# A two-layer decoder step: the seam from attention heads to the output units in another order, and the last memory mix inside the first key unit

## The chip, the core and the metric

The kernel runs on one core of a Trainium2 chip. Its engines are TensorE (PE in the rows; PEld is its weight load), VectorE (DVE), ScalarE (ACT), GpSimd (POOL) and SyncE (SP), which here issues DMAs. The metric is the device time of one execution in microseconds (us).

## What is computed

A trunk of two layers with width 1024 handles 544 tokens: 512 of a prompt and 32 of eight requests (four each). The part that matters here, cut from the reference:

```python
# layer 1, after the residual stream x of layer 0
k_new = rope(rmsnorm(x) @ w_k); v_new = rmsnorm(x) @ w_v
z = rmsnorm(x) @ w_in[1]; z_mix, z_mem = z[..., :768], z[..., 768:]
q = rope(z_mix)
p = softmax(q k / 8)                      # two score maps for each of 6 heads
o = (p[0] - lam * p[1]) @ v
o = rmsnorm(o, subln) * (1 - lam_init)    # per head, 128 wide
x = x + concat(o, memattn(z_mem)) @ w_out[1]
x = x + relu(rmsnorm(x) @ w_mlp1[1])**2 @ w_mlp2[1]
```

## The kernel before, in words

All matrix products with weights run in "units". A unit is one 128-wide slice of output features for all 544 tokens: eight contraction tiles (kt), for each of them three products (high weights by high and low operand, low weights by high operand), each in two token halves of 272. That is 48 matmuls. Unit j uses PSUM banks 2(j%2) and 2(j%2)+1. There are 186 units in one sequence; the ones here are the input units of layer 1 (`U_IN1`), 6 key units (`U_K`), 6 value units (`U_V`), 8 output units (`U_OUT1`) and the units of the second MLP. Weights come by DMA into one of four `weights_raw` slots; ScalarE writes the high part (L815), VectorE the low part (L1093) into one of two `weights_split` slots. So the weights of unit u+2 can be split only when unit u is done, and unit u+2 waits for `weight_lo`. VectorE also drains each unit's PSUM (`unit_out`), and in an output unit it adds the residual (L1116); ScalarE then makes the next operand and its square (L822, L827) ahead of the high part of the weights.

Each engine runs its instructions in the order in which the code is written; semaphores tie the engines together. The memory attention of layer 1 is ten items that are laid between the input units; `turn` transposes probabilities, `mix` multiplies them by values (L609), `items_drain` (L1212) empties bank 7. The last mix, of item 19, stands between the last input unit and the first key unit.

Queries and keys are rotated (rope). GpSimd starts four DMAs that swap lanes (`rotate`, L1531); it multiplies the queries itself (L1600 to L1602), and starts the DMAs of the keys after that and after the last key unit. VectorE waits for those (`k_swapped`) between the drain of value unit 0 and the drain of value unit 1, and multiplies the keys between the drains of the value units (L1428 to L1430).

The 28 items of the heads follow (24 of the prompt, 4 of the requests). Their scores use banks 0 to 5 in three slots, `turn` bank 6, `mix` bank 7 (L627). `mix_new` (L665) multiplies the requests' new values; it stands ahead of the last mix. After that comes the seam. The squared norm of each head is taken (POOL clamps, ACT squares, DVE `means`), the root is taken on ACT (L1062, which loads a table first), DVE scales the heads (L1249), PE transposes them into PSUM (`turn_head`, L783), ACT writes the high part (`head_high`, L1054) and DVE the rest (L1462) into `operand_a`. The request tokens have a path of their own (matmuls L789 and L790, `means` on 192 columns, L1452 to L1454, L1458). PE starts the output units when the rests of heads 0 to 2 and of the request tokens are there.

## Time and profile before

| | us |
|---|---|
| median of 3 runs | 1274.88 (1273.76 to 1275.64) |
| the profiled execution | 1276.16 |
| its span, first to last instruction | 1274.0 |
| PE busy | 1223.7 (96% of the span) |
| DVE / ACT / POOL busy | 572.0 / 409.4 / 347.8 |
| first seam (last input unit to key units) | about 639 to 643 |
| second seam (heads to output units) | about 802 to 838 |

Times in the rows count from the start of the span. A timeline row merges neighbouring instructions of one line and gives their start, duration and number; the bracket says how long the engine stood idle before the first and what released it. fp32 matmuls of the attention stand in the timeline as two for each one in the program. The clock in a window row is the granted TensorE clock, with 1.00 for 2.4 GHz and 0.50 for 1.2 GHz. The rows themselves stand in a section of their own.

### The profile page before, as it was taken

The page shows a single profiled execution, that of the slowest core. Times are in us where ns is not written, and L with a number is a line of the kernel's source. Part 1 is how long each engine was busy: PE and PEld are TensorE (multiplying, and loading weights), DVE is VectorE, ACT ScalarE, POOL GpSimd, SP SyncE. Part 2 cuts the span into 40 slices and gives each one's busy share as a digit, 9 for nine tenths or more (in the row PEclk, how much of TensorE's full clock was granted, in tenths as well). Part 3 has the DMA queues.
Part 4 walks back from the last instruction along what each step waited for, and adds up shares of the span by engine and source line. Part 5 has one row for each costly group of instructions (what it writes and reads, how often), then busy time and mean ns, then how long its engine had stood idle before and what let it go on. Part 6 is the DMA issues. An engine that isn't in the chain of part 4 may idle for free.

```text
span 1274.0 us, 23371 instructions
## 1 busy us (share of the span) xinstructions
PE 1223.7 (96%) x9674; PEld 1175.5 (92%) x9674; DVE 572.0 (45%) x856; ACT 409.4 (32%) x756; POOL 347.8 (27%) x284
## 2 busy tenths in 40 slices
PE   6998999999999999999999999699999999999997
PEld 6877999999999999998899866599999999999997
DVE  7667544333333333356634767645333333333334
ACT  7545332212212212344412366533222222212221
POOL 3363124205305305320054200012401511511521
PEclk9999999999999999999999999899999999999998
DMA  7624422332222322322344456022222332232221
GB/s 282 211 86 128 120 83 83 84 98 85 83 89 88 89 85 85 92 89 84 134 119 125 155 194 232 1 67 94 90 83 83 86 97 83 83 100 83 83 67 70
DMA packets 38032, 132.97 MB, mean 104 GB/s; under 512 B 4178, under 2 KB 7122, under 8 KB 37298
## 3 DMA queue, kind: packets, MB, share of 16 engines
q1 hardware_dynamic: 36834, 123.42, 30.8%
q0 software_dynamic: 1104, 8.15, 2.1%
q8 instruction: 76, 1.25, 0.4%
q14 instruction: 18, 0.15, 0.0%
HBM read 121.18 MB, written 7.03 MB: 101 GB/s over the span
## 4 chain that ended last, share of the span: by engine, by line
PE 90%; DVE 6%; ACT 2%; issue 1%; DMA 0%; POOL 0%; DVEq 0%; SPq 0%; ACTq 0%
PE psum L450 81%; DVE weights_split L1093 1%; DVE inv_rms L1112 1%; PE psum L550 1%; PE psum L627 1%; ACT weights_split L815 1%; PE psum L553 1%; PE psum L536 1%; PE psum L563 1%; PE psum L609 1%; PE psum L583 0%; PE psum L567 0%; PE psum L495 0%; PE psum L589 0%; DVE tiny L1197 0%
## 5 line engine op out<-in xcount | busy, mean ns | idle before, releaser
L450 PE MATMUL psum<-operand_b,weights_split 128*128 128x272 f32 x4416 | 564.2, 290 | 4.1 <-DVE weights_split L1093 3.9
L450 PEld LDWEIGHTS psum<-operand_b,weights_split 128*128 128x128 f32 x4416 | 558.2, 189 | 9.1 <-DVE weights_split L1093 4.9
L450 PE MATMUL psum<-operand_a,weights_split 128*128 128x272 f32 (+1 forms) x4068 | 522.3, 290 | 21.8 <-DVE weights_split L1093 14.3
L450 PEld LDWEIGHTS psum<-operand_a,weights_split 128*128 128x128 f32 x4068 | 515.4, 190 | 27.9 <-issue 20.5
L815 ACT ACTIVATE weights_split<-weights_raw 128x1024 fp32r<-128x1024 f32 (+1 forms) x186 | 192.8, 1037 | 388.5 <-PE psum L450 388.5
L1093 DVE TENSOR_TENSOR weights_split<-weights_raw,weights_split 128x1024 fp32r<-128x1024 f32 (+1 forms) x186 | 239.5, 1288 | 138.1 <-ACT weights_split L815 138.0
L1516 POOL TENSOR_TENSOR squares<-staging 128x544 f32<-128x544 f32 x64 | 76.4, 1194 | 471.5 <-ACT operand_b L861 207.6
L1147 DVE TENSOR_TENSOR residual<-psum,residual 128x544 f32<-128x544 f32 x48 | 34.8, 725 | 176.0 <-PE psum L450 176.0
L1128 DVE SCALAR_TENSOR_TENSOR staging<-psum,inv_rms 128x544 f32<-128x544 f32 x56 | 40.6, 725 | 150.1 <-PE psum L450 150.1
L1509 POOL TENSOR_TENSOR squares_sum<-squares_sum,squares 128x544 f32<-128x544 f32 (+1 forms) x35 | 48.5, 1386 | 115.8 <-ACT squares L827 115.2
L1518 POOL TENSOR_TENSOR operand_a<-squares,operand_a 128x544 fp32r<-128x544 f32 x32 | 65.0, 2032 | 2.5
L1518 POOL TENSOR_TENSOR operand_b<-squares,operand_b 128x544 fp32r<-128x544 f32 x32 | 64.9, 2028 | 2.5
L861 ACT ACTIVATE operand_b<-staging 128x544 fp32r<-128x544 f32 x24 | 15.9, 661 | 109.9 <-DVE staging L1128 109.9
L861 ACT ACTIVATE operand_a<-staging 128x544 fp32r<-128x544 f32 x24 | 15.9, 661 | 109.9 <-DVE staging L1128 109.9
L1116 DVE TENSOR_TENSOR residual<-psum,residual 128x544 f32<-128x544 f32 x31 | 22.5, 725 | 57.8 <-PE psum L450 57.8
L1197 DVE TENSOR_REDUCE tiny<-psum 128x2 f32<-128x512 f32 (+3 forms) x40 | 30.7, 769 | 18.2 <-PE psum L553 9.2
L827 ACT ACTIVATE squares<-residual 128x544 f32<-128x544 f32 x39 | 25.2, 647 | 30.9 <-DVE residual L1116 30.9
L822 ACT ACTIVATE operand_a<-residual,params 128x544 fp32r<-128x544 f32 x16 | 12.0, 753 | 64.1 <-DVE residual L1116 64.1
L891 ACT ACTIVATE staging<-psum 128x512 f32<-128x512 f32 (+4 forms) x48 | 22.5, 468 | 26.5 <-PE psum L589 22.5
L1509 POOL TENSOR_TENSOR squares_sum<-squares 128x544 f32<-128x544 f32 (+1 forms) x6 | 8.2, 1363 | 83.1 <-ACT squares L827 83.1
L822 ACT ACTIVATE operand_b<-residual,params 128x544 fp32r<-128x544 f32 x24 | 17.8, 742 | 36.7 <-DVE residual L1116 36.7
L877 ACT ACTIVATE probs_l<-psum,tiny 128x256 f32<-128x256 f32 x36 | 16.8, 472 | 39.6 <-DVE tiny L1205 39.6
(210 smaller groups left out, 719.4 us busy)
## 6 DMA issues: line engine op xcount, KB each, us to landing
weights_raw<-in_weights SPq DMA_DIRECT2D x180, 512.0 KB, 3.6
cache_tiles<-in_page_k SPq DMA_DIRECT2D x16, 384.0 KB, 4.0
cache_tiles<-in_page_v SPq DMA_DIRECT2D x16, 384.0 KB, 4.0
cache_tiles<-in_mem_k SPq DMA_DIRECT2D x8, 512.0 KB, 4.8
cache_tiles<-in_mem_v SPq DMA_DIRECT2D x8, 512.0 KB, 6.2
residual<-in_x SPq DMA_DIRECT2D x1, 2176.0 KB, 11.8
rotated<-projected POOLq DMA_DIRECT2D x4, 408.0 KB, 7.4
rotated<-keys POOLq DMA_DIRECT2D x4, 408.0 KB, 8.3
```

The costliest lines, as they stand in the source:

```text
L450: mm = pe.matmul(ps[:, 2 * (j % PS) + hf, 0:n], w(wr), act[:, ar, k, hf * n:(hf + 1) * n], start=(q == 0 and wr == 0 and ar == 0), stop=(q ...
L815: act.activation(split[:, s % HL, 0, 0:n], raw[:, s, 0:n], ACT.Copy).then_inc(weight_hi, 1)
L822: act.activation(dst, src, ACT.Copy, scale=gain(g, k)).then_inc(norm_hi, 1)
L827: act.activation(SQ[:, k % 2, 0:cols], src, ACT.Square).then_inc(sq_ready, 1)
L861: act.activation(hidden[:, 0, j, :], T[:, j % TS, :], ACT.Square).then_inc(hid_hi, 1)
L1093: dve.tensor_tensor(split[:, s % HL, 1, 0:n], raw[:, s, 0:n], split[:, s % HL, 0, 0:n].bitcast(F32), ALU.subtract).then_inc(weight_lo, 1)
L1128: dve.scalar_tensor_tensor(out=halves(T[:, j % TS, :]), in0=unit_psum(j), scalar=0.0, in1=halves(rms[:, :]), op0=ALU.max, op1=ALU.mult).th ...
L1147: dve.tensor_tensor(halves(X[:, j, :]), unit_psum(j), halves(X[:, j, :]), ALU.add)\
L1197: own.chain(dve.tensor_reduce(mx[:, s, :], sc[:, :, 0:n_keys], AX.X, ALU.max))
L1509: pool.tensor_tensor(sq_sum[:, 0:cols], a, SQ[:, k % 2, 0:cols], ALU.add).then_inc(sq_summed, 1)
L1516: pool.tensor_tensor(sq, t, t, ALU.mult).then_inc(hid_sq, 1)
L1518: pool.tensor_tensor(hidden[:, 1, j, :], sq, hidden[:, 0, j, :].bitcast(F32), ALU.subtract)\
```

## The change

First seam: the mix of memory item 19 is no longer ahead of key unit 0 but in its middle (`mid`, after contraction tile 3). On PE before (units L450, transposes L583, memory mixes L609):

```order
L583 MATMUL psum<-constants,probs_l_1_86 128x128 x4
L609 MATMUL psum<-staging,mem_values 64x128 x8
L450 MATMUL psum<-operand_b,weights_split 128x272 x384
L773 MATMUL psum<-constants,staging 128x128 x4
L774 MATMUL psum<-constants,staging 32x128
```

and after (the same lines are L451, L584 and L610 there):

```order
L584 MATMUL psum<-constants,probs_l_1_86 128x128 x4
L610 MATMUL psum<-staging,mem_values 64x128 x4
L451 MATMUL psum<-operand_b,weights_split 128x272 x24
L610 MATMUL psum<-staging,mem_values 64x128 x4
L451 MATMUL psum<-operand_b,weights_split 128x272 x360
```

Four of the eight memory mixes, those of item 19, now stand behind 24 matmuls of the key unit.

Second seam: `turn_head` of heads 0 and 1 moves into the attention loop, ahead of the transposes of item 46; `mix_new` goes behind the last mix and into another bank; the table of the root is loaded by a one-element root on ACT ahead of the copy of item 47; the heads are transposed into banks 2 to 7; the two matmuls of the requests' norm share bank 1. Output units 0 and 1 are written out as `first_units`: first the halves of tokens 0 to 271 of both units, contraction tile by contraction tile, each tile as soon as its head's rest is there, then the other halves of unit 0 and of unit 1. On PE before, from the mix of item 44 on (L589 transposes, L627 mixes, L665 `mix_new`, L783 head transposes, L789 and L790 the requests' norm, L450 units):

```order
L627 MATMUL psum<-values,staging 128x128
L589 MATMUL psum<-constants,probs_heads_88 128x128 x3
L627 MATMUL psum<-values,staging 128x128 x2
L589 MATMUL psum<-constants,staging 128x128 x4
L627 MATMUL psum<-values,staging 128x128 x3
L665 MATMUL psum<-probs_new,values_new 128x32 x6
L627 MATMUL psum<-values,staging 128x128 x4
L783 MATMUL psum<-constants,attention_out 128x128 x8
L789 MATMUL psum<-squares,ones 128x192
L790 MATMUL psum<-squares,ones 128x192
L783 MATMUL psum<-constants,attention_out 128x128 x16
L450 MATMUL psum<-operand_a,weights_split 128x272 x384
```

and after, from the transposes of heads 0 and 1 on (L674 head transposes, L590, L628, L666, L792, L793 as above, L799 half units):

```order
L674 MATMUL psum<-constants,attention_out 128x128 x8
L590 MATMUL psum<-constants,probs_heads_88 128x128 x3
L628 MATMUL psum<-values,staging 128x128 x2
L590 MATMUL psum<-constants,staging 128x128 x4
L628 MATMUL psum<-values,staging 128x128 x7
L666 MATMUL psum<-probs_new,values_new 128x32 x6
L674 MATMUL psum<-constants,attention_out 128x128 x8
L792 MATMUL psum<-squares,ones 128x192
L793 MATMUL psum<-squares,ones 128x192
L799 MATMUL psum<-operand_a,weights_split 128x272 x12
L674 MATMUL psum<-constants,attention_out 128x128 x8
L799 MATMUL psum<-operand_a,weights_split 128x272 x84
```

The last mix now stands ahead of `mix_new`, and the 96 matmuls of units 0 and 1 are L799, with the transposes of heads 4 and 5 after the first 12.

On DVE the seam reads, before (L1235 to L1237 `means` of the requests, L1243, L1244 factors, L1249 scaling, L1452 to L1454 the requests' scaling, L1462 rests of heads, L1458 rest of the requests):

```order
L1235 TENSOR_SCALAR staging<-psum 128x192
L1236 TENSOR_SCALAR staging<-psum 128x192
L1237 SCALAR_TENSOR_TENSOR staging<-staging 128x192
L1243 RECIPROCAL tiny<-tiny 128x8
L1244 TENSOR_TENSOR tiny<-tiny 128x8
L1249 TENSOR_TENSOR attention_out<-attention_out,tiny 128x512 x2
L1452 RECIPROCAL staging<-staging 128x192
L1453 TENSOR_TENSOR staging<-staging 128x192
L1454 TENSOR_TENSOR projected<-projected,staging 128x6x32
L1462 SCALAR_TENSOR_TENSOR operand_a<-psum,tiny,operand_a 128x512 x3
L1458 SCALAR_TENSOR_TENSOR operand_a<-projected,tiny,operand_a 128x6x32
L1462 SCALAR_TENSOR_TENSOR operand_a<-psum,tiny,operand_a 128x512 x3
```

and after (L1481 rests of heads, L1275 and L1276 factors, L1281 scaling, L1266 to L1269 `means`, L1495 to L1497 the requests' scaling):

```order
L1481 SCALAR_TENSOR_TENSOR operand_a<-psum,tiny,operand_a 128x512
L1275 RECIPROCAL tiny<-tiny 128x8
L1276 TENSOR_TENSOR tiny<-tiny 128x8
L1281 TENSOR_TENSOR attention_out<-attention_out,tiny 128x512 x2
L1481 SCALAR_TENSOR_TENSOR operand_a<-psum,tiny,operand_a 128x512
L1266 TENSOR_SCALAR staging<-psum 128x192
L1267 TENSOR_SCALAR staging<-psum 128x192
L1268 TENSOR_SCALAR staging<-psum 128x192
L1269 SCALAR_TENSOR_TENSOR staging<-staging 128x192
L1481 SCALAR_TENSOR_TENSOR operand_a<-psum,tiny,operand_a 128x512 x2
L1495 RECIPROCAL staging<-staging 128x192
L1496 TENSOR_TENSOR staging<-staging 128x192
```

The rests of heads now begin ahead of the factors and lie between the other steps; the rest of the requests is the last of all and has its own semaphore.

The diff, cut to its core:

```diff
+TURN_BANK = (2, 3, 4, 5, 6, 7)
@@ PE
             def mix_new(n):
                 pe.wait_ge(copied, DEC[-1] + 1)
-                pe.wait_ge(exped, n)
+                pe.wait_ge(exped, n + 1)
                 for h in range(HEADS):
-                    mm = pe.matmul(ps[:, head_bank(n - 1), SAMPLE * h:SAMPLE * (h + 1)]
+                    mm = pe.matmul(ps[:, head_bank(n), SAMPLE * h:SAMPLE * (h + 1)]
...
@@ PE, attention
+                    if n == n1 - 2:
+                        pe.wait_ge(exped, n1 - 2)
+                        turn_head(0)
+                        turn_head(1)
                     turn(n)
                     if n > n0:
                         mix(n - 1)
-                    if n == n1 - 1:
-                        mix_new(n)
                 mix(n1 - 1)
+                mix_new(n1 - 1)
...
-            mix(FIRST_HEAD - 1)
             for j in range(MIXT):
-                unit(U_K + j, j, B, ready=normed(G_KV) if j == 0 else None)
+                unit(U_K + j, j, B, ready=normed(G_KV) if j == 0 else None,
+                     mid=(lambda: mix(FIRST_HEAD - 1)) if j == 0 else None)
...
+            turn_head(2)
+            turn_head(3)
             pe.wait_ge(squared, QT * HEADS + 1)
...
+            def first_units(u):
+                def rows(j, hf, k):
+                    for wr, ar in ((0, 0), (0, 1), (1, 0)):
+                        mm = pe.matmul(ps[:, 2 * j + hf, 0:HALF], split[:, j, wr, lo_of(k)],
+                                       A[:, ar, k, hf * HALF:(hf + 1) * HALF], start=(k == 6 and wr == 0 and ar == 0),
                                       stop=(k == HEADS - 1 and wr == 1))
+                    return mm
+                pe.wait_ge(weight_lo, u + 2)
+                pe.wait_ge(cat_lo, 2)
+                for j in range(2):
+                    if j == 0:
+                        pe.wait_ge(new_added, 1)
+                    else:
+                        pe.wait_ge(mix_lo, MIXT + 1)
+                    rows(j, 0, 6)
+                    rows(j, 0, 7)
+                turn_head(4)
+                pe.wait_ge(drained, len(ITEMS))
+                turn_head(5)
+                for h in range(HEADS):
+                    pe.wait_ge(mix_lo, MIXT + h + 1)
+                    for j in range(2):
+                        rows(j, 0, h)
+                pe.wait_ge(sample_lo, 1)
+                for j in range(2):
+                    for k in (6, 7, 0, 1, 2, 3, 4, 5):
+                        mm = rows(j, 1, k)
+                    mm.then_inc(unit_done, 1)
+            first_units(U_OUT1)
+            for j in range(2, KT):
+                unit(U_OUT1 + j, j, A, kts=(6, 7, 0, 1, 2, 3, 4, 5))
@@ ACT, attention
+                    if n == n1 - 1:
+                        own.step(act.activation(tiny[:, 13:14], epsc, ACT.Sqrt))
+                    if n == n1 + 2:
+                        act.wait_ge(mixed, len(ITEMS))
+                        act.wait_ge(v_stored, 32)
+                        head_high(0)
@@ ACT, after the heads
-            act.wait_ge(v_stored, 32)
-            head_high(0)
+            for h in range(1, 5):
+                head_high(h)
             act.wait_ge(sub_mean, 4)
             act.activation(small[0], small[1], ACT.Sqrt, bias=eps_sub, scale=SUB).then_inc(sub_root, 1)
-            for h in range(1, HEADS):
-                head_high(h)
+            head_high(5)
@@ DVE
+            head_rest(0)
             head_factors(EARLY, QT * HEADS, 2)
             for h in range(EARLY_HEADS, HEADS):
                 scale_head(h)
+            head_rest(1)
+            dve.wait_ge(sub_mm, 1)
+            means(ps[:, 1, 0:NS], ps[:, 1, NS:2 * NS], small[1], small[2], small[3])
+            head_rest(2)
+            head_rest(3)
...
+            head_rest(4)
+            head_rest(5)
...
+               .then_inc(sample_lo, 1)
```

## Rows read from the trace of the kernel before

**Rows 1.** Waits of PE, whole span: engine, line, waited for: us, times, longest.

```profile
PE psum L450 <- issue: 3.9, 2, 3.7
...
PE psum L609 <- DVE projected L1212: 3.0, 2, 2.4
```

**Rows 2.** Timeline, first seam: start, us, engine, line, operation [idle before <-releaser].

```profile
642.08 0.66 PE L609 MATMUL psum<-staging,mem_values 128*64 128x128 f32 x8 [2.43 <-DVE projected L1212]
...
642.67 13.57 PE L450 MATMUL psum<-operand_b,weights_split 128*128 128x272 f32 x94
...
650.52 0.72 DVE L1414 TENSOR_TENSOR keys<-psum,inv_rms 128x544 f32<-128x544 f32 x1 [7.45 <-PE psum L450]
```

**Rows 3.** Windows: length, PE busy (matmuls), granted clock, DMA share, GB/s.

```profile
130.50:132.30 1.80, 0.09 (x2) 1.00 0.36 143
132.30:136.00 3.70, 3.70 (x30) 1.00 0.79 189
639.60:642.10 2.50, 0.07 (x4) 1.00 0.44 94
642.10:646.50 4.40, 4.40 (x26) 0.61 1.01 240
```

**Rows 4.** Timeline of POOL: the rotations of queries and keys.

```profile
651.79 2.33 POOL L1600 TENSOR_TENSOR rotated<-rotated,cos_sin 128x544 f32<-128x544 f32 x1 [9.78 <-DMA rotated<-projected]
...
681.89 2.01 POOL L1531 DMA_DIRECT2D rotated<-keys  x4 [0.82 <-DVE keys L1414]
```

**Rows 5.** Timeline, value units 1 to 3: VectorE and PE.

```profile
694.90 0.73 DVE L1428 TENSOR_TENSOR rotated<-rotated,cos_sin 128x544 f32<-128x544 f32 x1 [5.92 <-DMA rotated<-keys]
...
696.95 0.72 DVE L1420 TENSOR_TENSOR staging<-psum,inv_rms 128x544 f32<-128x544 f32 x1
697.58 1.22 DVE L1093 TENSOR_TENSOR weights_split<-weights_raw,weights_split 128x1024 fp32r<-128x1024 f32 x1
...
699.43 6.27 PE L450 MATMUL psum<-operand_b,weights_split 128*128 128x272 f32 x48
```

**Rows 6.** DMA issues, 640 to 652 us: tiles, queue, count, KB, us to landing.

```profile
weights_raw<-in_weights SPq DMA_DIRECT2D x1, 512.0 KB, 10.9
```

**Rows 7.** DMA issues, 681.5 to 695 us.

```profile
weights_raw<-in_weights SPq DMA_DIRECT2D x2, 512.0 KB, 9.4
```

**Rows 8.** Timeline of PE at the end of the heads.

```profile
806.20 0.55 PE L589 MATMUL psum<-constants,probs_heads 128*128 128x128 f32 x3 [1.82 <-DVE probs_heads L1179]
...
807.92 1.11 PE L589 MATMUL psum<-constants,staging 128*128 128x128 f32 x4 [0.33 <-DVE staging L1179]
...
810.22 1.52 PE L665 MATMUL psum<-probs_new,values_new 32*128 32x32 f32 x12
811.67 1.16 PE L627 MATMUL psum<-values,staging 128*128 128x128 f32 x8
...
819.15 1.26 PE L783 MATMUL psum<-constants,attention_out 128*128 128x128 f32 x8 [1.37 <-DVE attention_out L1249]
824.15 2.15 PE L450 MATMUL psum<-operand_a,weights_split 128*128 128x272 f32 x8 [3.74 <-issue]
```

**Rows 9.** Timeline of ACT: the table of the root.

```profile
815.05 1.28 ACT L1062 ACT_TABLE_LOAD   x1
```

**Rows 10.** Timeline of VectorE: head norm and rests.

```profile
814.36 0.17 DVE L1234 TENSOR_SCALAR tiny<-tiny 128x8 f32<-128x8 f32 x1 [0.52 <-ACT squares L903]
...
816.77 0.36 DVE L1234 TENSOR_SCALAR staging<-psum 128x192 f32<-128x192 f32 x1 [1.90 <-PE psum L790]
...
823.97 2.06 DVE L1462 SCALAR_TENSOR_TENSOR operand_a<-psum,tiny,operand_a 128x512 fp32r<-128x512 f32 x3
```

**Rows 11.** Timeline, ends of output units 0 and 1: VectorE.

```profile
831.80 0.72 DVE L1116 TENSOR_TENSOR residual<-psum,residual 128x544 f32<-128x544 f32 x1 [5.78 <-PE psum L450]
...
834.85 1.23 DVE L1093 TENSOR_TENSOR weights_split<-weights_raw,weights_split 128x1024 fp32r<-128x1024 f32 x1 [0.71 <-ACT weights_split L815]
...
837.82 0.72 DVE L1116 TENSOR_TENSOR residual<-psum,residual 128x544 f32<-128x544 f32 x1 [1.75 <-PE psum L450]
```

57 lines of the change are left out of this document (21 added, 36 removed).

## Prediction

> **What bounds the kernel now.** PE is busy for 96% of the span, so I read first who makes PE wait, then the timeline around each wait, then the granted clock. The waits of PE over the whole span name the two seams: 3.7 us with no releaser shown ahead of a unit, and 2.4 us of a memory mix for a drain by VectorE [rows 1]. The long one is the start of output unit 0 at 824.15 us [rows 8]. "issue" there hides a wait on a semaphore: the code lets PE go once three heads and the requests have their rests, and VectorE begins its last three head rests at 823.97 [rows 10], just behind that of the requests. The other is the mix of memory item 19 at 642.08 [rows 2]. In both a full pipe of 48-matmul units stands behind the waiting instruction, so what is taken away there is taken from the end, unless a later wait takes it back. Around a wait the clock matters as much: PE idle from 639.65 to 642.1 is followed by 4.4 us at 0.61 [rows 3]. The first key unit ends at about 650.5 instead of 6.0 us after its start at 642.7 [rows 2], so this low spell costs some 1.8 us. A wait of 1.7 us (130.6 to 132.3) with dense units on both sides was not followed by a low clock [rows 3].
>
> **Prices of a unit.** Output unit 1 takes 837.82 - 831.80 = 6.02 us at full clock [rows 11], 0.125 us a matmul. At half clock it would be 12.
>
> **First seam: the mix in key unit 0.** Nothing is added or removed; four memory mixes (0.66 us in 8 halves of instructions [rows 2]) go behind 24 matmuls. Key unit 0 can start at 639.65 and its first half ends at 642.7, when the drain that the mix waits for has been there for 0.7 us. So the wait of 2.43 us goes [rows 2], and with it the low clock of 1.8 us: PE is 4.2 us earlier through key units 1 to 5 and value unit 0. The splits of the weights hang on `unit_done` and move with PE.
>
> What is late next is the rotation of the keys. It is started by GpSimd when its own work on the queries is done, and that chain began at 640.0 whatever PE does afterwards. GpSimd was idle for only 0.82 us ahead of the start at 681.89 [rows 4], so the keys can start 0.8 us earlier at most. The weight load that follows the split for key unit 2 now runs 4.2 us earlier, at about 648.8, into the end of the query rotation, which can cost up to that 0.8 us again; I take the start as unchanged. The transfer itself took 13.0 us from first issue to VectorE's use (681.89 to 694.90 [rows 4, 5]), with two weight loads beside it [rows 7]; that of the queries, of the same size, took 11.8 (2.01 for the issues and 9.78 of waiting [rows 4]) with one beside it [rows 6]. With PE earlier, one of the two loads falls ahead of the rotation. So the keys land 1.2 us earlier, not 4.2. Behind them VectorE has three multiplications, the drain of value unit 1 and the low weights of unit 3, which ended at 697.58 + 1.22 = 698.8 [rows 5] and now end at 697.6. PE, which began unit 3 at 699.43 [rows 5], would be ready at 695.2 and starts at 697.65: of 4.2 us, 1.8 are left, and PE idles for 2.4 us. That is the very length that cost a low spell at the first seam; 1.7 us did not [rows 3]. By the nearer row I charge the 1.8 us again: **nothing** is left. The bounds: keys 1.9 us earlier and full clock give 2.5 us; keys no earlier (0.6 us left) and a low spell give -1.2 us. From there to the last heads the order is unchanged, and all moves along.
>
> **Second seam.** I follow it in the times of the trace of before.
>
> Transposes of heads 0 and 1: eight, 1.26 us for as many in the last row of their kind [rows 8]. PE was idle for 1.82 us ahead of 806.20 [rows 8]; they fit in and cost nothing. Without that cover they would cost 1.26.
>
> The table of the root: 1.28 us of load [rows 9] plus some 0.25 for the one-element root, now between ACT's copies of items 46 and 47, 807.3 to 808.8. The next copy waits for the transposes of item 47, which end at 807.92 + 1.11 = 809.0 [rows 8]: hidden by 0.2 us. If these ran at full clock they would end at 808.5 and the load would cost 0.3.
>
> `mix_new` behind the last mix: before, 810.22 to 811.67, then the mix to 812.8 [rows 8]. Now the mix starts when the drain of item 46 ends (810.7) and ends at 811.8, 1.0 us earlier; `mix_new` ends at 813.25. So the heads' squares are ready 1 us earlier, and the requests' sum is added at 813.6, as before. VectorE is free for the norm at 814.0.
>
> From there VectorE sets the pace. Before, it went from 813.84 to 823.97 + 2.06 = 826.0 with two waits, 0.52 and 1.90 us [rows 10]: 12.2 - 2.4 = 9.8 us of work. The change adds no work to it and fills both waits with rests, since ACT's root needs no table and the high parts are there. So it ends near 814.0 + 9.8 = 823.8, plus some 0.3 for an added drain of its pipe at each turn: rest of head 5 at 823.8, that of the requests at 824.2.
>
> PE in that time: transposes of heads 2 and 3 (1.3 to 1.8 us), the requests' sums (1.7 at the clock of before), 12 matmuls of memory features (1.5), transposes of heads 4 and 5 (1.3), which end at about 819.5, then 24 matmuls of heads 0 to 3 (3.0) until 822.6. It then waits half a us for head 4 and finishes the first halves at 823.8 + 0.75 = 824.6. The second halves are 48 matmuls: unit 0 is done at 827.6, unit 1 at 830.6. Before, it was 831.8 and 837.8 [rows 11].
>
> The new wait: unit 2 needs unit 0's slot of split weights. From unit 0's end to the end of that split took 834.85 + 1.23 - 831.8 = 4.3 us [rows 11]: residual, operand, square, high part, low part. Before, unit 1 ran for 6.0 us and hid it. Now unit 1 ends 3.0 us behind unit 0, so PE waits 1.3 us and starts unit 2 at 831.9. Units 3 and later have 6 us cover again. Gain at unit 2: 837.8 - 831.9 = **5.8 us**. The 1.3 us wait is shorter than the 1.7 us that left the clock alone [rows 3]; if it does bring a low spell, 1.8 go, leaving 4.0. If the last mix runs at full clock throughout, another 1.0 comes: 6.8.
>
> **Sum.** 0.0 + 5.8 = 5.8 us. The span goes from 1274.0 to 1268.2, the profiled time from 1276.16 to 1270.4. The profiled execution was 1.3 us over the median, so the median goes from 1274.88 to 1269.1. The bounds added up: 4.0 - 1.2 = 2.8 and 6.8 + 2.5 = 9.3, so 1272.1 to 1265.6.
>
> **A rule beside the rows.** Moving transposes into an idle stretch might also keep the clock up there. The transposes and mix of item 47 ran low (four transposes 1.11 us [rows 8]); at full clock they would take half of that, and the seam would begin up to 1.0 us sooner. The rows have no stretch of transposes alone to judge by, so my sum leaves it out. By the Trainium skill (TensorE: Matmul & The Clock Gate, Part 4: PE-mode transpose) a transpose does not count as busy for the gate in the same way: by it the total stays 5.8; were it wrong, 6.8. No run so far shows which.
>
> **Rivals.**
> 1. The keys' rotation doesn't bind (it lands 4 us earlier, by less DMA traffic): the first seam keeps 4.2, total 10.0, 1264.9 us. Against it stands GpSimd's chain, idle for 0.82 us only [rows 4].
> 2. The clock stays low through the first halves, because the work there comes in pieces. Then 12 matmuls take 3.0, transposes 1.8, 36 matmuls 9.0: first halves end at 830.5, unit 1 at 836.5, and unit 2 waits until 837.8. Nothing is gained: 1274.8. For it: the 8 transposes at 813.27 and what follows ran low in before, and PE's low spells come where work is thin. Against it: work is dense from 819 on, and the low spell behind the first seam ended among dense units, within a stretch of 4.4 us [rows 3].
> 3. Slower: the spell lasts through the second halves too. Unit 0 is done at 836.5, unit 1 at 842.5, 4.7 us behind before: 1279.5 us. In rival 2 PE has 1.3 us to spare ahead of unit 2; so it gets slower than before once more than 10 of the 48 second-half matmuls run low as well. The row of 642.10 speaks against it: among dense matmuls the clock came back.
> 4. The half units don't start early, because one of the rests (heads or the requests) is late. If heads 4 and 5 come at 826 as before, unit 0 is done at 829.8 and unit 2 starts at 834.1: 3.7 gained, inside my range.
>
> **How the numbers follow.** Forecast with its bounds 0.77; rival 1 0.08; rival 2 or something that leaves less than 2.5 us 0.10; rival 3 0.05. The range that holds 8 in 10 takes the bounds and the spread of the runs (0.9 us each way at most): 1265.0 to 1272.6. A measurement of this kernel can tell about 0.2%, 2.5 us, from no change. Faster 0.85, same 0.10, slower 0.05.
>
> **What would show it.** Right: no wait of PE ahead of the memory mix, key unit 1 about 4 us earlier; the keys landing near 693.7 and a wait of about 2 us in front of value unit 3, then a low window; no table load behind the heads; `mix_new` after the last mix; no VectorE wait over 0.5 us between 814 and 824; a wait of about 1.3 us in front of output unit 2, which starts 5 to 7 us earlier than 837.8. Wrong: value unit 3 begins 4 us earlier (rival 1); a granted clock of half past the transposes of heads 4 and 5 (rivals 2 and 3); ACT's copy of item 47 waiting for the table; or a second wait at output unit 3.

## The result, and the profile after

The changed kernel takes 1264.16 us (median of 4 runs, 1263.82 to 1266.52), beside 1275.26 (4 runs, 1273.76 to 1277.67) for the kernel before on the same chip. The ratio is 0.9918, with a 95% interval of 0.99 to 0.9936: it is faster, by 11.1 us or 0.8%. The forecast was 5.8 us and 1269.1; the time lies 0.8 us below the low end of the range.

| | before | after |
|---|---|---|
| median of the runs together | 1275.26 | 1264.16 |
| profiled execution | 1276.16 | 1264.18 |
| its span | 1274.0 | 1262.1 |
| PE busy in it | 96% | 1215.8 us, 96% |

**First seam.** In the timeline of PE after (start, us, line, operation, idle before and its releaser) the memory mix of item 19 stands inside key unit 0 and waits for nothing, where before it waited 2.43 us [rows 2]:

```profile
636.30 0.66 PE L610 MATMUL psum<-staging,mem_values 128*64 128x128 f32 x8
636.89 3.26 PE L451 MATMUL psum<-operand_b,weights_split 128*128 128x272 f32 x24
640.08 0.66 PE L610 MATMUL psum<-staging,mem_values 128*64 128x128 f32 x8
```

POOL starts the keys' rotation after 0.30 us of idle (0.82 before [rows 4]), and its transfer has landed when VectorE's next rows begin:

```profile
678.52 2.00 POOL L1570 DMA_DIRECT2D rotated<-keys  x4 [0.30 <-POOL projected L1641]
```

```profile
690.14 0.73 DVE L1460 TENSOR_TENSOR rotated<-rotated,cos_sin 128x544 f32<-128x544 f32 x1 [7.69 <-DMA rotated<-keys]
...
692.18 0.72 DVE L1452 TENSOR_TENSOR staging<-psum,inv_rms 128x544 f32<-128x544 f32 x1
692.81 1.22 DVE L1125 TENSOR_TENSOR weights_split<-weights_raw,weights_split 128x1024 fp32r<-128x1024 f32 x1
```

Value unit 3 still waits behind that chain, in two pieces: for the drain (0.34 us, with the turn of the decode tiles) and for the split of its weights (0.36). Its 48 matmuls then run at full clock:

```profile
692.95 0.66 PE L783 MATMUL psum<-constants,staging 128*128 128x128 f32 x4 [0.34 <-DVE staging L1452]
693.44 0.27 PE L784 MATMUL psum<-constants,staging 128*32 128x128 f32 x1
694.08 6.30 PE L451 MATMUL psum<-operand_b,weights_split 128*128 128x272 f32 x48 [0.36 <-DVE weights_split L1125]
```

**Second seam.** The timeline of PE from the last heads on. L674 is `turn_head`, L628 x8 at 804.34 the last mix, L666 `mix_new`, L799 the two half units, L451 a whole unit:

```profile
797.20 0.55 PE L658 MATMUL psum<-constants,staging 128*128 128x128 f32 x3 [1.44 <-ACT staging L950]
...
798.75 1.04 PE L674 MATMUL psum<-constants,attention_out 128*128 128x128 f32 x8
800.74 0.55 PE L590 MATMUL psum<-constants,probs_heads 128*128 128x128 f32 x3 [0.95 <-DVE probs_heads L1211]
...
802.48 0.66 PE L590 MATMUL psum<-constants,staging 128*128 128x128 f32 x4 [0.70 <-DVE staging L1211]
...
804.34 1.13 PE L628 MATMUL psum<-values,staging 128*128 128x128 f32 x8 [0.54 <-DVE attention_out L1255]
805.40 1.52 PE L666 MATMUL psum<-probs_new,values_new 32*128 32x32 f32 x12
806.85 1.09 PE L674 MATMUL psum<-constants,attention_out 128*128 128x128 f32 x8
...
809.00 1.82 PE L799 MATMUL psum<-operand_a,weights_split 128*128 128x272 f32 x12
810.65 1.04 PE L674 MATMUL psum<-constants,attention_out 128*128 128x128 f32 x8
811.44 3.31 PE L799 MATMUL psum<-operand_a,weights_split 128*128 128x272 f32 x24
816.33 7.79 PE L799 MATMUL psum<-operand_a,weights_split 128*128 128x272 f32 x60 [1.58 <-DVE operand_a L1481]
825.48 2.77 PE L451 MATMUL psum<-operand_a,weights_split 128*128 128x272 f32 x20 [1.35 <-DVE weights_split L1125]
```

The turns of heads 0 and 1 fill what was an idle 1.82 us [rows 8]; the four transposes of item 47 take 0.66 us where they took 1.11; the first halves begin at 809.00, and are dense but for 1.58 us of waiting for head 4's rest ahead of the last twelve of them (the x60 are these and the 48 of the second halves). Unit 2 starts at 825.48, after 1.35 us of waiting for the low part of its weights. On ACT the table load stands between two copies of the items, and the copy behind it starts 0.1 us after the transposes' end (802.48 + 0.66):

```profile
801.83 1.28 ACT L943 ACT_TABLE_LOAD   x1
803.13 0.20 ACT L943 ACTIVATE tiny<-tiny 128x1 f32<-128x1 f32 x1
803.24 0.58 ACT L918 ACTIVATE staging<-psum 128x512 f32<-128x512 f32 x1
```

VectorE's chain from the requests' square to the last rest, and then the drains and the split that unit 2 waits for:

```profile
807.41 0.26 DVE L1474 TENSOR_SCALAR staging<-projected 128x192 f32<-128x192 f32 x1
...
815.54 1.40 DVE L1481 SCALAR_TENSOR_TENSOR operand_a<-psum,tiny,operand_a 128x512 fp32r<-128x512 f32 x2
816.86 0.41 DVE L1501 SCALAR_TENSOR_TENSOR operand_a<-projected,tiny,operand_a 128x192 fp32r<-128x192 f32 x1
821.16 0.72 DVE L1148 TENSOR_TENSOR residual<-psum,residual 128x544 f32<-128x544 f32 x1 [3.90 <-PE psum L799]
...
824.20 1.23 DVE L1125 TENSOR_TENSOR weights_split<-weights_raw,weights_split 128x1024 fp32r<-128x1024 f32 x1 [0.71 <-ACT weights_split L842]
```

From the norm's first step (807.59, just behind the first row) to 816.86 + 0.41 = 817.27 it is 9.7 us with no wait shown, where before two waits lay in it [rows 10].

**Where the 11.9 us between the two spans lie.** I divide both traces at four points: M, the start of PE's memory mix of item 18; V4, the start of value unit 4; D, the start of the last three decode transposes (L657 before, L658 after); U2, the start of the first matmul of output unit 2. (Where units 0 and 1 are whole, that is the 97th matmul from unit 0's start, at 837.62 us before. The expectations count to the end of unit 1 there, 0.15 us later, and so have 35.1 for 35.0.)

| stretch | before | after | difference |
|---|---|---|---|
| start to M, ahead of any change | 638.99 | 636.30 | 2.69 |
| M to V4, first seam | 67.02 | 64.38 | 2.64 |
| V4 to D, order unchanged | 96.64 | 96.52 | 0.12 |
| D to U2, second seam | 34.97 | 28.28 | 6.69 |
| U2 to the end | 436.41 | 436.62 | -0.21 |

So 2.7 us of the difference come from a stretch in which nothing is changed. The granted clock falls for a while at some idle places of PE in one execution and not in the next, and before's trace had two such low spells (near 55 and near 196 us) that after's has not: this share is luck. A single pair of traces is not enough here. The experiments therefore repeat both kernels, and each is read by the two stretches M to V4 and D to U2 as well as by its time.

### The profile page after: what moved, and what is told of

It is laid out like the page before. It is cut to its first block, busy times and chain, and to the rows that moved or that the text cites. A ratio compares the mean times of both kernels' runs of the same rounds, so it can differ in the third digit from the quotient of the medians.

```text
span 1262.1 us, 23371 instructions
## 1 busy us (share of the span) xinstructions
PE 1215.8 (96%) x9674; PEld 1167.6 (93%) x9674; DVE 572.7 (45%) x856; ACT 408.7 (32%) x757; POOL 347.5 (28%) x284
## 4 chain that ended last, share of the span: by engine, by line
PE 85%; DVE 7%; POOL 3%; ACT 2%; DMA 2%; issue 1%; DVEq 0%; SPq 0%; ACTq 0%; POOLq 0%
PE psum L451 76%; DVE weights_split L1125 1%; DVE inv_rms L1144 1%; PE psum L551 1%; PE psum L628 1%; ACT weights_split L842 1%; DMA rotated<-projected 1%; DMA rotated<-keys 1%; POOL projected L1640 1%; POOL projected L1641 1%; PE psum L554 1%; PE psum L537 1%; POOL rotated L1639 1%; PE psum L564 1%; PE psum L610 1%
## 5 line engine op out<-in xcount | busy, mean ns | idle before, releaser
L451 PE MATMUL psum<-operand_b,weights_split 128*128 128x272 f32 x4416 | 561.2, 289 | 4.5 <-DVE weights_split L1125 4.3
L451 PEld LDWEIGHTS psum<-operand_b,weights_split 128*128 128x128 f32 x4416 | 555.1, 189 | 9.8 <-DVE weights_split L1125 5.6
L451 PE MATMUL psum<-operand_a,weights_split 128*128 128x272 f32 (+1 forms) x3972 | 507.9, 289 | 19.6 <-DVE weights_split L1125 16.1
L451 PEld LDWEIGHTS psum<-operand_a,weights_split 128*128 128x128 f32 x3972 | 500.9, 190 | 25.7 <-issue 16.8
L1672 POOL TENSOR_SCALAR squares<-attention_out 128x128 f32<-128x128 f32 x24 | 7.0, 293 | 77.9 <-DVE attention_out L1255 74.9
```

Source lines behind the costliest of these rows:

```text
L451: mm = pe.matmul(ps[:, 2 * (j % PS) + hf, 0:n], w(wr), act[:, ar, k, hf * n:(hf + 1) * n], start=(q == 0 and wr == 0 and ar == 0), stop=(q ...
```

## The experiments

All were run with the kernel before beside them on the same chip; its medians there were 1274.31 (25 runs, e1 to e4), 1275.2 (14 runs, r_after, e7 to e9), 1275.32 (13 runs, b, e5, e6) and 1275.52 (11 runs, c). The stretches of all traces, with the mean granted clock of the 12 us behind D (b_before1, b_before2, c2 and c1 had one execution each; the other times are medians):

| kernel | time, us | M to V4 | D to U2 | clock behind D |
|---|---|---|---|---|
| before, first trace | 1275.26 | 67.02 | 35.0 | 0.81 |
| b_before1, before | 1276.11 | 67.00 | 38.1 | 0.56 |
| b_before2, before | 1272.83 | 67.01 | 34.9 | 0.72 |
| c2_before3, before | 1270.2 | 65.50 | 34.1 | 0.86 |
| e1_seam1_only | 1273.57 | 67.47 | 38.1 | 0.56 |
| e2_seam2_only | 1267.41 | 67.01 | 28.3 | 0.86 |
| after, first trace | 1264.16 | 64.38 | 28.3 | 1.00 |
| r_after, after | 1264.24 | 66.97 | 28.3 | 0.86 |
| c3_after3, after | 1265.84 | 65.02 | 28.25 | 0.91 |
| e3_no_halves | 1270.29 | 66.86 | 34.6 | 0.84 |
| e4_keys_later | 1265.77 | 63.18 | 28.3 | 0.86 |
| e5_table_late | 1265.58 | 63.76 | 29.6 | 0.86 |
| e6_new_first | 1265.85 | 64.19 | 28.6 | 0.86 |
| e7_turns_late | 1268.12 | 63.72 | 32.3 | 0.57 |
| c1_turns_late2 | 1266.14 | 65.03 | 30.0 | 0.86 |
| e8_unit0_first | 1264.47 | 63.90 | 27.1 | 0.86 |
| e9_both | 1263.31 | 63.18 | 30.3 | 0.58 |
| c4_both2 | 1262.31 | 63.18 | 27.0 | 0.86 |

V4 to D is 96.4 to 96.8 in every one, and U2 to the end 435.4 to 436.6, but for 437.8 in e7.

### e1_seam1_only: only the mix in key unit 0

```diff
 (before.py)
-            mix(FIRST_HEAD - 1)
             for j in range(MIXT):
-                unit(U_K + j, j, B, ready=normed(G_KV) if j == 0 else None)
+                unit(U_K + j, j, B, ready=normed(G_KV) if j == 0 else None,
+                     mid=(lambda: mix(FIRST_HEAD - 1)) if j == 0 else None)
```

> The kernel before with the first seam of the change alone: the last memory mix of layer 1 inside key unit 0, nothing else. Theory (the keys' rotation takes most of the gain back): the mix's 2.4 us wait is gone and key unit 1 ends 4 us earlier where the clock was low before, but value unit 3 waits for the weights behind the keys; gain about 2 to 3 us, time about 1272.5. Rival A (the rotation does not bind): 4.2 us, about 1271. Rival B (the clock falls again at value unit 3): 0 to 1 us.

Measured: 1273.57 us (12 runs) beside 1274.31, ratio 0.999 (0.9973 to 1.0007), no difference that can be told. The timeline of PE at value unit 3:

```profile
695.42 0.66 PE L773 MATMUL psum<-constants,staging 128*128 128x128 f32 x4 [1.92 <-DVE staging L1420]
...
696.55 6.69 PE L450 MATMUL psum<-operand_b,weights_split 128*128 128x272 f32 x39 [0.37 <-DVE weights_split L1093]
```

PE waited for the keys' chain for 1.92 + 0.37 us, and a low spell followed: 39 matmuls in 6.69 us, where full clock gives 0.13 us each. This is the picture of the prediction for this seam and rival B of the expectation, not the 2 to 3 us of its theory: M to V4 is longer, if anything (67.47 against 67.02). The trace also has a long low spell behind D, where its order is that of before; it is of one of the slowest executions, 1277.08 us.

### e2_seam2_only: the mix of item 19 back ahead of the key units

```diff
 (after.py)
+            mix(FIRST_HEAD - 1)
             for j in range(MIXT):
-                unit(U_K + j, j, B, ready=normed(G_KV) if j == 0 else None,
-                     mid=(lambda: mix(FIRST_HEAD - 1)) if j == 0 else None)
+                unit(U_K + j, j, B, ready=normed(G_KV) if j == 0 else None)
```

> The changed kernel with the last memory mix of layer 1 back ahead of the key units: the second seam alone. Theory: from the end of the heads' requests item to the start of output unit 2 it takes 28.4 us in place of before's 35.1, a gain of 6.8 us; time about 1268.5. If the missing part of the forecast lies in the second seam, the gain is 8 us or more (1267 or less); if it lies in the first seam or elsewhere, it is 6 to 7.

Measured: 1267.41 us (8 runs), ratio 0.9942 (0.9921 to 0.9962): 6.9 us of gain. The mix waits as it did before, and the second seam has all of its gain (28.3 us from D to U2):

```profile
640.57 0.66 PE L610 MATMUL psum<-staging,mem_values 128*64 128x128 f32 x8 [2.43 <-DVE projected L1244]
```

So most of the gain is the second seam's. The two parts alone give 0.7 and 6.9 us in time, together 7.6, where the whole change gave 9.7 to 11.1 in its three sets of runs; with medians that move by 2 us this is no evidence of anything between the parts.

### e3_no_halves: output units 0 and 1 as whole units

```diff
 (after.py)
-            def first_units(u):
-                ...
-            first_units(U_OUT1)
-            for j in range(2, KT):
+            turn_head(4)
+            pe.wait_ge(drained, len(ITEMS))
+            turn_head(5)
+            pe.wait_ge(cat_lo, 2)
+            pe.wait_ge(new_added, 1)
+            pe.wait_ge(sample_lo, 1)
+            for j in range(KT):
                 unit(U_OUT1 + j, j, A, kts=(6, 7, 0, 1, 2, 3, 4, 5))
```

> The changed kernel with output units 0 and 1 as whole units again, started when all rests are there; the rest of the change stays. Theory (PE works through the wait for the rests): the 48 matmuls of the first halves come behind the rests, while the wait of 1.35 us at unit 2 goes; unit 2 starts at about 817.3 + 12.0 = 829.3 of the changed trace in place of 825.5: 3.8 us slower than the changed kernel, about 1268. Rival (the earlier norm and the clock carry the gain, not the halves): less than 1 us slower.

Measured: 1270.29 us (12 runs), ratio 0.9966 (0.995 to 0.9982), 4.0 us of gain. PE stands still until the last rest:

```profile
812.46 1.97 PE L674 MATMUL psum<-constants,attention_out 128*128 128x128 f32 x8 [0.21 <-DVE attention_out L1255]
820.07 8.11 PE L451 MATMUL psum<-operand_a,weights_split 128*128 128x272 f32 x45 [5.64 <-issue]
```

The unit behind the idle 5.64 us shows 45 matmuls in 8.11 us, some 2.2 more than at full clock: the turns ahead of the gap already ran low (1.97 us for eight), and the clock is still low behind it. The halves are worth 34.6 - 28.3 = 6.3 us in the traces, some 4 without that spell, and 4.5 to 6 in the medians. A part of that isn't the halves' own: whole units here wait for the requests' rest, which stands last of all, where before's waited for it and three heads only.

### e4_keys_later: VectorE takes the rotated keys one value unit later

```diff
 (after.py, in VectorE's value units)
-                if j == 0:
+                if j == 1:
                     dve.wait_ge(k_swapped, 64)
-                for h in ([j] if j < 4 else [4, 5] if j == 4 else []):
+                for h in ([0, 1] if j == 1 else [j] if j in (2, 3) else [4, 5] if j == 4 else []):
```

> The changed kernel with VectorE's wait for the rotated keys moved behind the drain of value unit 1 and the low weights of unit 3 (the multiplications of heads 0 and 1 then follow together). Theory (value unit 3 waits for what stands behind the rotated keys on VectorE): the two PE waits of 0.34 and 0.36 us and the late transposes between value units 2 and 3 go, 1.0 us faster than the changed kernel. Rival (the work only moves, and the multiplications end later than value unit 5): no change or slower.

Measured: 1265.77 us (6 runs), ratio 0.9927 (0.9903 to 0.9951). PE goes through value units 2 and 3 without a wait:

```profile
692.74 0.60 PE L783 MATMUL psum<-constants,staging 128*128 128x128 f32 x4
...
693.20 6.26 PE L451 MATMUL psum<-operand_b,weights_split 128*128 128x272 f32 x48
```

M to V4 is 63.18 us, here and in e9_both and c4_both2 which have the same edit, to the hundredth each time. That is the floor of the seam: the three traces of the changed kernel stand 1.2, 1.8 and 3.8 us over it. So what is left of the first seam is the keys' chain and the low spell that it sometimes brings. In time the expected 1.0 us does not show: 1265.77 is 8.5 us under before, where the changed kernel was 9.7 to 11.1 under it.

### r_after: the changed kernel again

> The changed kernel again, beside more runs of the one before. The parts by themselves gave 1.3 us (first seam) and 7.4 us (second), 8.7 together, where the four runs of the result gave 11.1. Theory (low clock spells come and go from execution to execution, and four runs had few): a median near 1265.5, gain about 9 us; in its trace the stretch from the last memory mix to value unit 4 is 64.4 us, or 66 to 67 with a low spell, and from the requests' last transposes to output unit 2 it is 28.3 us. Rival (the two seams help each other): 1264 again, gain 11.

Measured: 1264.24 us (5 runs, 1263.27 to 1269.87), ratio 0.9924 (0.99 to 0.9947). That is the rival's 1264, not the 1265.5 of the theory, though the traces below name another reason than two seams that help each other. The same program as in the first trace, and at value unit 3 another picture:

```profile
694.36 0.66 PE L783 MATMUL psum<-constants,staging 128*128 128x128 f32 x4 [1.43 <-DVE staging L1452]
...
695.49 7.68 PE L451 MATMUL psum<-operand_b,weights_split 128*128 128x272 f32 x47 [0.37 <-DVE weights_split L1125]
```

Here the wait is 1.43 + 0.37 us and a low spell follows, as the prediction had it (47 matmuls in 7.68 us). At 0.34 + 0.36 us in the first trace none did. Ten traces have the mix inside key unit 0 and the keys where the changed kernel has them (after three times, e1, e3, e5 to e8, c1). In them the first of the two waits is 0 (three times), 0.17, 0.34, 1.00, 1.03, 1.31, 1.43 and 1.92 us. In the first seven the unit takes 6.3 us, in the last three (e3, r_after, e1) it runs low and takes 7.8. The difference comes from when the keys land: VectorE's first use of them lies 53.2 to 55.4 us behind M, in the very order of these waits.

At the second seam a low spell begins here too, but it falls on the eight transposes in the gap (1.04 us in the first trace) and is over before item 47:

```profile
801.67 1.91 PE L674 MATMUL psum<-constants,attention_out 128*128 128x128 f32 x8
```

### e7_turns_late and c1_turns_late2: turns of heads 0 and 1 behind the last mix

```diff
 (after.py)
-                    if n == n1 - 2:
-                        pe.wait_ge(exped, n1 - 2)
-                        turn_head(0)
-                        turn_head(1)
                     turn(n)
                     ...
                 mix(n1 - 1)
+                turn_head(0)
+                turn_head(1)
                 mix_new(n1 - 1)
```

> The changed kernel with the transposes of heads 0 and 1 behind the last mix instead of in the gap ahead of item 46. Theory: the gap of 1.8 us on PE is back, 1.0 us of transposes comes onto the path of the new requests' sum, and ACT, which makes head 0's high part ahead of the last squares, is about 1.5 us late: the norm starts 1 to 1.5 us later, time 1 to 2 us over the changed kernel. A low spell that begins in the gap then falls on items 46 and 47, as before the change (another 1 us). Rival (VectorE's chain covers them): less than 0.5 us.

> The transposes of heads 0 and 1 behind the last mix once more, for its trace. Theory (the idle gap draws the low spell out): a low clock of 6 us or more between the requests' last transposes and the requests' norm, mean clock under 0.7 over the 12 us behind those transposes, and 30 us or more to output unit 2. Rival (long spells come by chance, 5 of 14 traces): one short spell, 0.85 or so, 29.5 us.

Measured: e7 1268.12 us (9 runs), ratio 0.9949 (0.993 to 0.9967), beside 1264.24 and 0.9924 for the changed kernel on the same chip; c1, one execution, 1266.14. D to U2 is 32.3 and 30.0 us against 28.3. e7 is 3.9 us over the changed kernel, where 1 to 2 (and 1 for a spell) were expected; c1 came out as its rival had it, with a short spell (0.86), against the theory of a long one under 0.7, though its 30.0 us are those of the theory. The timeline of PE in c1, with the idle gap open again:

```profile
801.76 0.73 PE L590 MATMUL psum<-constants,probs_heads 128*128 128x128 f32 x3 [1.82 <-DVE probs_heads L1209]
...
803.49 1.11 PE L590 MATMUL psum<-constants,staging 128*128 128x128 f32 x4
...
806.24 1.13 PE L628 MATMUL psum<-values,staging 128*128 128x128 f32 x8 [0.54 <-DVE attention_out L1253]
807.21 1.04 PE L674 MATMUL psum<-constants,attention_out 128*128 128x128 f32 x8
```

The last mix starts 8.02 us behind D, as the prediction had it for the changed kernel (8.05); in after it is 7.14. Of c1's 1.7 us, about half are that, and the other half the eight transposes that now stand on the path. The other 2.3 us of e7 are a longer low spell. The granted clock (the number behind the count in brackets) of the 12 us behind D in e7, in c1 and in after:

```profile
796.97:808.97 12.00, 9.36 (x42) 0.57 0.00 1
```

```profile
798.22:810.22 12.00, 9.06 (x57) 0.86 0.00 1
```

```profile
797.20:809.20 12.00, 8.93 (x65) 1.00 0.01 2
```

The surest mark is the four transposes of item 47, the row `staging 128*128 128x128 x4` of L589 or L590. With the gap ahead of item 46 empty they take 1.11 or 1.12 us, half clock, in seven traces of seven (before four times, e1, e7, c1). With the gap filled they take 0.66 in ten of eleven; the one with 1.12 is e9_both. It is not that no spell comes: by the granted clock in short windows, one begins 1.3 to 1.6 us behind D in eight of the eleven, and runs over the eight transposes (1.86 to 1.92 us), but it ends at 4.7 to 5.0, ahead of item 47 at 5.27. With the gap idle, the four that begin so early (b_before1, b_before2, e1, e7) last to 8.0 us or beyond, and the other three begin at 3.4 to 4.1, and run over item 47.

### b_before1, b_before2 and c2_before3: the kernel before again

> The kernel before once more, for its trace. Theory (a spell of low clock on the path of the second seam comes in nearly every execution of the kernel before, and its length varies): from the requests' last transposes to output unit 2 it takes 35 to 38 us, where four traces with the new second seam took 28.3 us in every one. Rival (the 35.1 us of the first trace were a bad one): 33.5 us or less without a spell, which would put the missing 2 us elsewhere.

> The kernel before a second time, for the spread. Theory and rival as for the first: 35 to 38 us, or 33.5 us and less, from the requests' last transposes to output unit 2; 67.0 us from the last but one memory mix to value unit 4 with a spell behind the first wait, 65.2 us without.

> The kernel before a third time, for its trace. Theory: low for 6 us or more again, 35 to 38.2 us from the requests' last transposes to output unit 2. Rival: 34 us or less.

Measured, one execution each: 1276.11, 1272.83 and 1270.2 us. c2 has the same 2.43 us wait ahead of the memory mix as before's first trace [rows 2], and no low spell behind it. The rows: the wait in c2, then the clock over 12 us in c2 and in b_before1:

```profile
639.49 0.66 PE L609 MATMUL psum<-staging,mem_values 128*64 128x128 f32 x8 [2.43 <-DVE projected L1212]
```

```profile
638.00:650.00 12.00, 10.51 (x87) 1.00 0.79 185
```

```profile
638.00:650.00 12.00, 10.11 (x71) 0.86 0.78 183
```

That alone is 1.5 us (65.50 against 67.0). At the second seam, 34.1 to 38.1 us: b_before1 and b_before2 as expected, c2 between its theory (35 or more) and its rival (34 or less). The window behind D, in b_before1, before's first trace and c2:

```profile
800.27:812.27 12.00, 9.89 (x44) 0.56 0.01 1
```

```profile
802.65:814.65 12.00, 8.94 (x52) 0.81 0.00 1
```

```profile
798.34:810.34 12.00, 8.68 (x52) 0.86 0.00 1
```

A second spell stands in all five traces with before's order here: the clock is low at the start of output unit 0, behind PE's 3.74 us of waiting. In b_before1, 30 matmuls take 6.26 us, where full clock gives some 3.9:

```profile
823.95 6.26 PE L450 MATMUL psum<-operand_a,weights_split 128*128 128x272 f32 x30 [3.74 <-issue]
```

From unit 0's start to U2 it is 13.5 us in before's first trace, 14.4, 13.9 and 13.7 in b_before1, b_before2 and c2, and 14.4 in e1, where two units at full clock take 12.0. So this spell costs before 1.4 to 2.4 us. The change takes the wait away, and the spell with it: no trace with the half units has a low clock from its second halves on.

The 25 runs of before beside e1 to e4, on one chip, lie between 1270.57 and 1279.81 us: a spread of 9.2 us, of the size of the gain.

### e5_table_late: no early root

```diff
 (after.py, ACT)
-                    if n == n1 - 1:
-                        own.step(act.activation(tiny[:, 13:14], epsc, ACT.Sqrt))
```

> The changed kernel without the early root: the table is loaded behind the heads again. Theory (the root is on VectorE's path): its 1.28 us hold up the root of the heads, from which VectorE has one head rest of 0.7 us as cover, and the high parts of heads 1 to 3 behind it; the stretch to output unit 2 grows from 28.3 to 29 to 29.5 us. Rival (covered by rests): under 0.3 us.

Measured: 1265.58 us (4 runs), ratio 0.9936 (0.9913 to 0.9958); D to U2 29.63 us, 1.35 more than after. The table is loaded at its first use, on ACT, and VectorE waits for the root behind it:

```profile
808.57 1.28 ACT L1093 ACT_TABLE_LOAD   x1
809.86 0.30 ACT L1093 ACTIVATE tiny<-tiny 128x8 f32<-128x8 f32 x1
```

```profile
810.19 0.20 DVE L1273 RECIPROCAL tiny<-tiny 128x8 f32<-128x8 f32 x1 [1.21 <-ACT tiny L1093]
```

The medians don't tell it from the changed kernel; the traces do. By the Trainium skill (ScalarE: Activation LUTs, What ACT_TABLE_LOAD costs) a switch costs the load of about 1.28 us and a drain of about 1.38 us besides. The load is 1.28 us here as well, but the root starts 0.01 us behind it, and the whole seam is 1.35 us longer: the second part isn't seen in this kernel.

### e6_new_first: `mix_new` ahead of the last mix

```diff
 (after.py)
-                mix(n1 - 1)
                 mix_new(n1 - 1)
+                mix(n1 - 1)
```

> The changed kernel with the matmuls of the requests' new values ahead of the last mix again. Theory: the last mix ends 1.45 us later, the last squares 1.3 us later, the sum of the requests 1.1 us earlier; the later one rules the norm, so the stretch to output unit 2 grows from 28.3 to about 29.2 us. Rival (the sum of the requests rules): it shrinks.

Measured: 1265.85 us (10 runs), ratio 0.9937 (0.9921 to 0.9953); D to U2 28.57 us, 0.3 more than after. The last mix starts at 806.54 instead of 7.14 us behind D (7.98), but 0.5 of the 0.8 us are absorbed behind it; 0.9 us more than after had been expected.

### e8_unit0_first, e9_both and c4_both2: unit 0 finished ahead of unit 1

```diff
 (after.py, first_units; e9 and c4 have e4's edit as well)
-                for h in range(HEADS):
+                for h in range(4):
                     pe.wait_ge(mix_lo, MIXT + h + 1)
                     for j in range(2):
                         rows(j, 0, h)
-                pe.wait_ge(sample_lo, 1)
+                pe.wait_ge(sub_mean, 4)
                 for j in range(2):
-                    for k in (6, 7, 0, 1, 2, 3, 4, 5):
+                    rows(j, 1, 6)
+                    rows(j, 1, 7)
+                for j in range(2):
+                    for h in (4, 5):
+                        pe.wait_ge(mix_lo, MIXT + h + 1)
+                        rows(j, 0, h)
+                    pe.wait_ge(sample_lo, 1)
+                    for k in range(HEADS):
                         mm = rows(j, 1, k)
                     mm.then_inc(unit_done, 1)
```

> The changed kernel with the 96 matmuls of output units 0 and 1 in another order: the 12 of the memory features' second halves while PE waits for head 4 (1.58 us), then all that is left of unit 0, then of unit 1. Theory (unit 2 starts 4.3 us behind the end of unit 0, whose weights' slot it needs): unit 0 ends 1.6 us earlier and unit 2 starts at 823.9 in place of 825.5 of the changed trace, 1.6 us faster. Rival (unit 2 is bound by unit 1's end): 1.2 us or less, or none if the first seam's or the spells' share moves against it.

> The order of e8 and the later wait for the keys of e4 together. Theory: both gains add, 1.0 + 1.6 = 2.6 us under the changed kernel, and the low spell at value unit 3 doesn't come since its wait is gone (1 us more on average): about 1262. Rival (one gain swallows the other, or spells move elsewhere): 1264 to 1265.

> The order of e9 (keys' wait later, unit 0 finished first) once more, on the chip of the changed kernel. Theory: 63.2 us from the last but one memory mix to value unit 4 and 27.1 us to output unit 2 without a long spell, 2 to 2.5 us under the changed kernel. Rival: no difference that can be measured, since spells of 1.7 us hide it.

Measured: e8 1264.47 us (5 runs), 0.9917 (0.99 to 0.9935); e9 1263.31 (6 runs), 0.9908 (0.9888 to 0.9927); c4, the same kernel, 1262.31 (6 runs), 0.9901 (0.9879 to 0.9923). In e8 the wait for head 4 is filled with twelve second-half matmuls, and the stretch to U2 is 1.2 us shorter:

```profile
812.43 11.47 PE L799 MATMUL psum<-operand_a,weights_split 128*128 128x272 f32 x84
825.24 4.02 PE L451 MATMUL psum<-operand_a,weights_split 128*128 128x272 f32 x30 [1.34 <-DVE weights_split L1132]
```

The wait ahead of unit 2 stays (1.34 us): unit 0 ends sooner, and unit 2 is still ready 4.3 us behind it. The expected 1.6 us are 1.2 in the trace and none in the medians (1264.47 beside 1264.24). e9 shows the long low spell behind D that before has, with the gap filled (clock 0.58); c4 doesn't (0.86), and is the shortest at both seams together.

### c3_after3: the changed kernel a third time

> The changed kernel once more. Theory (the gap is filled): no spell or one short one behind the requests' last transposes, 28.3 us to output unit 2; median 1264 to 1266, 9 to 11 us under the kernel before. Rival: a long spell and 30 us or more as often as with the gap.

Measured: 1265.84 us (6 runs), ratio 0.9931 (0.9908 to 0.9953). Beside it on the same chip c4 is 3.5 us faster; on another chip e9 was 0.9 faster than r_after. Over all, the changed kernel has 15 runs with median 1264.7 and the variant 12 with 1262.3: both edits together give about 2 us more than the change. The intervals of the two ratios overlap on each chip, but both hold before's spread; of c4's six runs, five are below all six of c3.

## Why the prediction was right or wrong

**The direction was right, and so was the path.** PE is bound at these two places, and what was taken from its waits there came off the end. The second seam carries the gain, the first nearly none (e1: no difference; e2: 6.9 us).

**The steps that failed** are three terms of the sum: "I charge the 1.8 us again: nothing is left" at the first seam (measured: 1.6 us left on average, the spell in three traces of ten); the start of the last mix, 8.05 us behind D (measured: 7.14); and before's side of the second seam, taken from one trace (measured: 1.0 us more on average). Beyond them, 2.6 us between the two profiled executions came from stretches without a change, which is luck: in the third set of runs the changed kernel took 1265.84 us, inside the range.

**First seam, 0.0 forecast, 1.6 measured.** The mean of M to V4 is 66.7 us over the five traces with the mix ahead of the key units and 65.1 over the ten with it inside. Right: no wait at the mix, PE about 4 us earlier at key unit 0's end, the keys' rotation as the next thing late, VectorE's five steps behind it (three multiplications, the drain, the split), PE waiting in two pieces, and the value unit 3 low in some. e4 shows the chain by taking the keys' wait away: 63.18 us always. Two terms under that step failed. "Start as unchanged" was 0.7 us off: the rotation starts 42.2 us behind M, before 42.9 [rows 4], near the 0.8 that I had given as the most; and it takes 11.6 us to VectorE's use (678.52 to 690.14; 10.8 to 12.6 in the ten traces) against 11.8 assumed and 13.0 before. So PE's wait ahead of unit 3, 2.4 us in the forecast, came out at 0.3 to 2.3 us, both parts together, and "I charge the 1.8 us again", which rests on the 2.4, charged a spell that comes in three of ten, where the wait is longest; it costs 1.5 us. On the other side of the sum the spell behind the 2.43 us wait is missing in c2. One trace gave each of these one value.

**Second seam, 5.8 forecast, 6.7 against the same trace, 7.7 on average.** In times behind D:

| step | before | forecast | after |
|---|---|---|---|
| last mix starts | 9.02 | 8.1 | 7.14 |
| VectorE free for the norm | 11.2 | 11.35 | 10.4 |
| PE ready for head 4 | | 19.95 | 17.55 |
| PE goes on with head 4 | | 20.45 | 19.13 |
| last rest done | 23.4 | 21.5 | 20.1 |
| unit 0 done | 29.15 | 24.95 | 23.96 |
| PE waits ahead of unit 2 | | 1.3 | 1.35 |
| unit 2 starts | 35.0 | 29.25 | 28.28 |

The first row is off, and the rows behind it are shifted by the same 0.9 to 1.4 us; unit 0's end and unit 2's start by 1.0. The work of VectorE, forecast at 9.8 us and 0.3 to 0.4 more for drains of its pipe, took 9.7; no run shows such an extra term. The shift is the bound "If the last mix runs at full clock throughout, another 1.0 comes". I took the other value, because no row showed transposes alone. c1 and e7 show what decides: with the turns out of the gap, the transposes of item 47 run at half clock and the mix starts 8.0 to 8.2 us behind D, as forecast. PE waits 1.58 us for head 4, not 0.5, because its transposes and the root's sums ran at full clock too and it is ready 2.4 us sooner than I said, VectorE 1.3.

The last 1.0 us lies in before, not in after. D to U2 is 35.0, 38.1, 34.9, 34.1 and 38.1 us in the five traces of before's order there (mean 36.0), and 28.25 to 28.3 in the five of the changed one (after three times, e2, e4). Before pays for a long low spell behind D in some executions (half of the 1.0), and for a longer spell at output unit 0 than its first trace had (1.9 us on average against 1.4, the other half). The forecast held the 1.4 without naming it, since it started from unit 2 of that trace. The five traces of the changed order have short spells (clock 0.86 or 0.91 in four of the five): they fall on work that waits for VectorE anyhow. A long one can come there too: e9 has the same order up to the second halves, and took 3.2 us more than c4.

**The rule beside the rows.** By the Trainium skill (TensorE: Matmul & The Clock Gate, Part 4: PE-mode transpose) a transpose doesn't count as busy for the gate in the same way; by that the total was to stay 5.8 us, and would be 6.8 otherwise. With eight transposes in the gap, item 47's ran at full clock in ten traces of eleven, without them in none of seven, and the stretch gave 6.7. The measurement goes against the rule as I had applied it. What the work in the gap did was to let the clock come back ahead of item 47, not to keep it up: mostly the eight transposes ran low themselves. That it was the transposes as such, and not PE's shorter idle time, is not shown; no run put other work into the gap.

**The sum.** 1.6 + 7.7 = 9.3 us; the medians give 9.7 to 11.1 in the three sets of runs with the changed kernel. The range was too narrow: its bounds came from one trace's spells, and 0.9 us were allowed for the spread of the runs, from three runs; 25 runs of before reach from 3.7 us below their median to 5.5 above it.

**Rivals.** Rival 1 gave nearly the measured time, 1264.9, and is refuted all the same: PE waits for the keys' chain in all traces without e4's edit, and e1 has none of its 4.2 us. Rivals 2 and 3 named a real thing, a low clock in this seam (0.57 in e7, 0.58 in e9), but it reached into the first halves by twelve matmuls at most (3.06 us in e7, 2.24 in c3, 1.8 at full clock elsewhere); the next 24 took 3.3 us. Rival 3 also gives PE 1.3 us to spare ahead of unit 2, which is wrong by the prediction's own 4.3 us: unit 2 follows the end of unit 0, so that each low matmul of unit 0 would have delayed it at once. Rival 4 did not come: rests end 817.27 - 797.20 = 20.1 us behind D, forecast 21.5.

**Parts that did little.** The early table is worth 1.35 us and was covered with nothing to spare: at full clock the transposes end as it ends, as the prediction's bound of 0.3 had it; 0.1 shows. The order of `mix_new` is worth 0.3.

## What to carry to other kernels

Where the granted clock of PE comes and goes between executions, take three or more traces of the kernel before, divide them at fixed points of the program, and give each low spell a chance and a length before it enters a sum. When a wait on an in-order engine is taken away, follow the chain that it hid to its next meeting with the engine: here five steps of VectorE behind a transfer took back most of 4 us. Small work in an idle gap can be worth more than its own time, if the work that follows would otherwise run at half clock.
